# Four weight pieces split on GpSimd in the fourth mixer, and attention scores of both query tiles ahead of their masks in the second and third

## The reference

```python
# second mixer: 8 heads, a part of 128 and a rotated part of 64 in each key
s = einsum(q_nope, k_nope) + einsum(q_rope, k_rope)        # chunk-wise causal mask
# third: 8 heads of two maps of 64 each, causal; softmax(map 0) - lambda * softmax(map 1)
s = einsum('bqhcd,bkhcd->bhcqk', qblk, k) * scale
# fourth: 16 query heads of 64 on 4 key heads, band of 128 keys, with a sink
s = einsum('bnqhgd,bnkhd->bnhgqk', qb, kw) / sqrt(64)
m = max(max(s), sink); e = exp(s - m); p = e / (sum(e) + exp(sink - m))
o = einsum('bnhgqk,bnkhd->bnqhgd', p, vw);  out = o.reshape(B, S, 1024) @ w_o
```

## Time and profile before

| | before |
|---|---|
| median of 3 runs | 1372.0 us (1371.38, 1372.0, 1374.17) |
| the profiled execution, its own time | 1369.26 us |
| its span in the trace | 1367.4 us |
| PE busy | 1337.3 us, 98% of the span |
| PE weight loads busy | 1134.0 us, 83% |
| DVE busy | 892.5 us, 65% |
| ACT busy | 714.7 us, 52% |
| POOL busy | 180.6 us, 13%, nearly all of it in the first 300 us |

### The profile page before, as it was taken

The page is one execution under the profiler, slowest core; times in us unless marked ns, Lnnn a source line. Parts: engine busy times, 40 slices in busy tenths (PEclk is TensorE's granted clock), DMA queues, the critical chain, the costliest instruction groups (busy, mean ns, idle before and its releaser), DMA issues.

```text
span 1367.4 us, 18921 instructions
## 1 busy us (share of the span) xinstructions
PE 1337.3 (98%) x7209; PEld 1134.0 (83%) x7209; DVE 892.5 (65%) x1539; ACT 714.7 (52%) x1217; POOL 180.6 (13%) x327
## 2 busy tenths in 40 slices
PE   9999998999999999999999999999999999999998
PEld 8899897878888888888888887888888877888887
DVE  7886876666555477575554699775554687755553
ACT  7766563345444356454443566564443566544441
POOL 1487888301100000000000000000000000000000
PEclk9999999999999999999999999999999999999999
DMA  9766543346665545266655365066655432566652
GB/s 251 191 160 167 154 123 124 96 126 207 185 189 185 177 145 197 62 201 185 186 186 193 128 210 161 26 210 186 187 188 191 155 123 63 178 192 186 187 191 82
DMA packets 171059, 223.24 MB, mean 163 GB/s; under 512 B 11649, under 2 KB 137402, under 8 KB 170970
## 3 DMA queue, kind: packets, MB, share of 16 engines
q1 hardware_dynamic: 166976, 213.03, 50.4%
q0 software_dynamic: 2224, 7.03, 2.1%
q10 hardware_dynamic: 1770, 1.99, 0.5%
HBM read 217.67 MB, written 4.33 MB: 162 GB/s over the span
## 4 chain that ended last, share of the span: by engine, by line
PE 79%; DVE 13%; ACT 3%; DMA 2%; issue 2%; SPq 0%; ACTq 0%; DVEq 0%
PE psum L959 23%; PE psum L961 22%; PE psum L960 22%; DVE w_low L706 4%; DMA ring<-in_gdn_w_in 2%; PE psum L1192 2%; PE psum L1186 2%; PE psum L1443 1%; PE psum L1403 1%; PE psum L1476 1%; DVE work L2646 1%; DVE arena L2761 1%; ACT w_high L692 1%; PE psum L950 1%; DVE work L878 1%
## 5 line engine op out<-in xcount | busy, mean ns | idle before, releaser
L706 DVE TENSOR_TENSOR w_low<-ring,w_high 128x1024 fp32r<-128x1024 f32 (+3 forms) x395 | 476.7, 1217 | 320.9 <-ACT w_high L692 320.6
L692 ACT ACTIVATE w_high<-ring 128x1024 fp32r<-128x1024 f32 (+3 forms) x395 | 410.6, 1048 | 421.4 <-PE psum L961 402.0
L959 PE MATMUL psum<-w_high,hT 128*128 128x512 f32 (+2 forms) x944 | 371.2, 393 | 0.0
L961 PE MATMUL psum<-w_high,hT 128*128 128x512 f32 (+2 forms) x944 | 366.1, 388 | 0.0
L960 PE MATMUL psum<-w_low,hT 128*128 128x512 f32 (+2 forms) x944 | 365.5, 387 | 0.0
L959 PE MATMUL psum<-w_high,parts 128*128 128x512 f32 (+1 forms) x532 | 210.4, 395 | 1.1 <-DVE parts L2769 1.1
L961 PEld LDWEIGHTS psum<-w_high,hT 128*128 128x128 f32 x944 | 177.2, 188 | 36.5
L961 PE MATMUL psum<-w_high,parts 128*128 128x512 f32 (+1 forms) x532 | 207.0, 389 | 0.0
L960 PE MATMUL psum<-w_low,parts 128*128 128x512 f32 (+1 forms) x532 | 206.8, 389 | 0.0
L960 PEld LDWEIGHTS psum<-w_low,hT 128*128 128x128 f32 x944 | 177.5, 188 | 33.8
L959 PEld LDWEIGHTS psum<-w_high,hT 128*128 128x128 f32 x944 | 177.4, 188 | 33.6
(11 more groups left out here) (303 smaller groups left out, 1395.4 us busy)
## 6 DMA issues: line engine op xcount, KB each, us to landing
ring<-in_ffn_w_gate_up SPq DMA_DIRECT2D x176, 256.0 KB, 3.3
ring<-in_w_gate_up SPq DMA_DIRECT2D x176, 256.0 KB, 3.2
ring<-in_gdn_w_in SPq DMA_DIRECT2D x48, 512.0 KB, 4.7
ring<-in_ffn_w_down SPq DMA_DIRECT2D x44, 512.0 KB, 3.3
ring<-in_w_down SPq DMA_DIRECT2D x44, 512.0 KB, 3.2
ring<-in_da_w_qkv SPq DMA_DIRECT2D x24, 512.0 KB, 4.1
ring<-in_gdn_w_out SPq DMA_DIRECT2D x16, 512.0 KB, 3.4
ring<-in_mla_w_out SPq DMA_DIRECT2D x8, 512.0 KB, 3.7
```

The source lines that it names most:

```text
L692: nc.scalar.activation(piece_slot(w_high, n), piece_slot(ring, n), ACT.Copy).then_inc(s.w_hi, 1)
L706: nc.vector.tensor_tensor(piece_slot(w_low, n), piece_slot(ring, n), piece_slot(w_high, n).bitcast(F32), ALU.subtract).then_inc(s.w_lo, 1)
L959: mm(out, lhs[0], rhs[0], start=start, stop=False)
L961: return mm(out, lhs[1], rhs[0], start=False, stop=stop)
```

## The change

Two things change. In the second and third mixer (`shades_last=True`, the default) a round's scores are issued as: products of both query tiles (in the second mixer the parts of 128 first, then those of 64), then all shades. The fourth mixer (`shades_last=False`) keeps tile 0 with its shades, then tile 1 with its. In the fourth mixer the four pieces named above are split by GpSimd, each by a copy and a subtraction, once `sw_rounds.max` has reached 4 (the maxima of round 3 are known). The four `split_high` of ScalarE and the four `split_low` of VectorE go; both engines wait ahead of their next split until GpSimd's are done.

```diff
-        sw_rounds = Rounds(sem, "sw", ..., HD, q_by)
+        sw_rounds = Rounds(sem, "sw", ..., HD, q_by, shades_last=False)
...
+                def products(i, t, n):
+                    u = i % 2
+                    for j in range(2):
+                        mm(B[2 * u + j][:, keys_of(t)], q(i, j, t)[n], k(i, j, t)[n], start=(n == 0 and (t == 0 or not A.shades_last)),
+                           stop=False, skip_group_check=A.shades_last)
...
+                    if A.shades_last:
+                        for n in parts_:
+                            for t in range(T):
+                                products(i, t, n)
+                        for t in range(T):
+                            last = shaded(i, t)
...
                 if i == 2:
                     empty_bank(act, tp_sq, 5, 1)
-                elif 3 <= i < 7:
-                    split_high(act, a_kv + 5 + i + SPLIT)
             attention(sw_rounds, True, beside_round, last_squares)
             empty_banks(act, tp_so, 1)
+            act.wait_ge(s.w_hi, POOL_SPLITS.stop)
...
                     query_roots(1)
-                elif i < 5:
-                    split_low(dve, a_kv + 5 + i + SPLIT)
-                elif i > 5:
-                    split_low(dve, a_kv + 4 + i + SPLIT)
...
+            dve.wait_ge(s.w_lo, POOL_SPLITS.stop)
...
+            pool.wait_ge(sw_rounds.max, 4)
+            for n in POOL_SPLITS:
+                pool.wait_ge(s.w_hi, n)
+                pool.wait_ge(w_ready[n % RING], landings(n))
+                pool.wait_ge(s.piece_used, n - SPLIT + 1)
+                copy(piece_slot(w_high, n), piece_slot(ring, n)).then_inc(s.w_hi, 1)
+                pool.wait_ge(s.w_hi, n + 1)
+                pool.wait_ge(s.w_lo, n)
+                tt(piece_slot(w_low, n), piece_slot(ring, n), piece_slot(w_high, n).bitcast(F32), ALU.subtract).then_inc(s.w_lo, 1)
```

More of the change, by code:

```diff
@@ L257, with __init__ @@
 class Rounds:
-    def __init__(self, sem, name, rounds, scale, masks, dv, by=None):
+    def __init__(self, sem, name, rounds, scale, masks, dv, by=None, shades_last=True):
         self.rounds, self.scale, self.masks, self.dv, self.by = rounds, scale, masks, dv, by
+        self.shades_last = shades_last
         self.scores = sem(f"{name}_scores")
@@ L453, in program @@
         ffns.append(add_ffn(3, a["w_gate_up_2"][1], a["w_down_2"][1]))
+        POOL_SPLITS = range(a_sout.first - 4 + SPLIT, a_sout.first + SPLIT)
         PROJECTIONS = [pr.first for pr in (a_gout, ffns[0].down, a_lout, ffns[1].down, a_dout, ffns[2].down, a_sout,
@@ L815, in program @@
         da_rounds = Rounds(sem, "da", DA_HEADS, HD ** -0.5, (None, shade_causal), 128)
-        sw_rounds = Rounds(sem, "sw", SW_HEADS // 2, HD ** -0.5, (shade_window, shade_causal), HD, q_by)
+        sw_rounds = Rounds(sem, "sw", SW_HEADS // 2, HD ** -0.5, (shade_window, shade_causal), HD, q_by, shades_last=False)
         def score_banks(u):
@@ L1436, in round_scores @@
             def round_scores(A, q, k):
-                def scores(i):
[L1439 to L1449, removed]
+                def products(i, t, n):
[3 more added lines that the diff above has]
+                           stop=False, skip_group_check=A.shades_last)
@@ new lines, in shaded @@
+                def shaded(i, t):
+                    u = i % 2
+                    for j in range(2):
+                        tiles_ = [(kt, A.masks[1 if kt == t else 0]) for kt in range(t + 1)]
+                        tiles_ = [(kt, shade) for kt, shade in tiles_ if shade is not None]
+                        for n, (kt, shade) in enumerate(tiles_):
+                            last = mm(B[2 * u + j][:, (t + kt) * P:(t + kt + 1) * P], ident_b, shade, start=False,
+                                      stop=(n == len(tiles_) - 1 and (t == T - 1 or not A.shades_last)), skip_group_check=A.shades_last)
+                    return last
@@ new lines, in scores @@
+                def scores(i):
+                    parts_ = range(len(q(i, 0, 0)))
+                    if A.shades_last:
[4 more added lines that the diff above has]
+                            last = shaded(i, t)
+                    else:
+                        for t in range(T):
+                            for n in parts_:
+                                products(i, t, n)
+                            last = shaded(i, t)
```

## The result

| | before | after |
|---|---|---|
| median of six runs each | 1372.21 us (1370.89 to 1374.17) | 1384.78 us (1383.06 to 1387.78) |
| ratio | | 1.0091, 95% interval 1.0078 to 1.0104 |
| span of the profiled execution | 1367.4 us | 1381.0 us |
| fourth mixer: first scores to projection, in the trace | 1116.93 to 1154.54, 37.61 us | 1116.58 to 1168.12, 51.54 us |

The change costs 12.6 us. I had predicted 6.6 (1378.6 us, range 1370 to 1384): the direction was right, the size was half, and the time lies above the upper end of my range. The last row shows where the time is. The fourth mixer is 13.93 us longer, and from its projection to the end of the span both traces need 212.86 and 212.88 us, so nothing behind it is late.

The account below looks back on a forecast made before the run. TensorE, busy 98% of the span, was taken as the bound, nearly even with ScalarE and VectorE in the fourth mixer. Terms 7.8 + 0.7 - 1.2 - 0.7 = 6.6 us over 1372.0 gave 1378.6 us, range 1370 to 1384.

Parts of the forecast that it names:

- stall: Fourth mixer: GpSimd's splits hold VectorE's small operations, so round 4's maxima end 7.8 us late, bounds 0 to 9.6.
- clock: Fourth mixer: TensorE's granted clock drops while it idles and stays low into later rounds, costing 0.7 us, 0 to 1.7.
- splits off ScalarE and VectorE: Fourth mixer: without these splits round 7's turns come sooner, 1.2 us gained, bounds 0.7 to 1.9.
- order of the scores: Second and third mixer: one half-array entry fewer per round, seven rounds counting, 0.7 us gained, 0 to 2.1.
- What bounds it: TensorE, busy 98% of the span; in the fourth mixer's rounds 4 to 6 TensorE, ScalarE and VectorE nearly even.
- the step on the copies: Fourth mixer: five of VectorE's thirteen small operations pass beside GpSimd's second copy; the last ends at 1140.4, not 1135.8.
- the upper bound: Fourth mixer: if copies hold VectorE too, two operations per GpSimd operation, round 4's maxima end at 1148, 9.6 us late.
- The step that the reciprocal would be held: Fourth mixer, round 2: GpSimd's third subtraction holds VectorE's reciprocal of `finished` until 1142.4.
- the first 3.4 us behind the stall: Fourth mixer: a low clock reaching into the rounds after the stall costs up to half of this length.
- No hold: Fourth mixer: GpSimd's long operations don't hold VectorE; only 1.9 us of gains remain, 1370.1 us; chance 0.17.
- VectorE slipping in more often: Fourth mixer: four or more VectorE operations pass between copy and subtraction; stall 2 to 4 us, 1372 to 1374.5; chance 0.10.
- the third rival: Fourth mixer: copies twice as long or VectorE held through subtraction and copy; stall 11 to 13, 1383 to 1387 us; chance 0.06.

Follow-up runs that it names:

- kernel 12: Changed kernel with 3, 46 and 5 unread identity products in TensorE's waits ahead of round 4's scores, round 3's values and round 4's turns; 1378.95 us.
- kernel 8: Changed kernel with GpSimd's splits started after all eight maxima, plus seven unread identity products ahead of round 4's scores and turns; 1368.69 us.
- kernel 11: Kernel before with only the scores' new order, plus seven unread identity products ahead of round 4's scores and turns; 1370.54 us.
- kernel 10: Changed kernel with GpSimd doing only the four copies and the four subtractions back on VectorE; 1381.72 us.
- kernel 5: Changed kernel with GpSimd's splits started once all eight maxima are known instead of the fourth; 1377.73 us.
- kernel 6: Changed kernel with GpSimd's splits started one round later, at the fifth maxima; 1377.92 us.
- kernel 9: Kernel before with only seven unread identity products added, ahead of round 4's scores and turns; 1370.68 us.
- kernel 1: Kernel before with only the scores' new order, splits left on ScalarE and VectorE; 1375.90 us.

## Why the prediction came out at half the loss

The lengths of the mixers in the traces split the loss into terms, each against the one predicted. The sum fell short by 5.8 us: 3.1 of the stall and 3.6 of the clock, less 0.8 that the order of the scores gave more.

| term | predicted us | measured us | from |
|---|---|---|---|
| stall | +7.8 (0 to 9.6) | +10.91 | kernel 12 less kernel 8, 47.29 - 36.38 |
| clock | +0.7 (0 to 1.7) | +4.25 | after less kernel 12, 51.54 - 47.29 |
| splits off ScalarE and VectorE | -1.2 (-1.9 to -0.7) | -1.23 | kernel 8 less kernel 11, 36.38 - 37.61 |
| order of the scores | -0.7 (-2.1 to 0) | -1.50 | second and third mixer, first scores to projection, after less before: 21.15 - 21.88 and 31.40 - 32.17 |
| sum | +6.6 | +12.4 | medians: +12.6 |

The two spans differ by 13.6 us. The 1.1 us that the terms leave is a later start of the second mixer in the trace of after (538.63 against 537.53), ahead of everything that the change touches.

**What bounds it, and the splits taken off.** Both right. Round 7's wait of 0.71 us behind ScalarE's split is gone (0.19 us at 1165.22), and the mixer gets 1.23 us shorter (kernel 8 against kernel 11).

**The stall: the mechanism was right, the step on the copies was wrong.** The hold lasts to the end of GpSimd's instruction, as predicted. The prediction let "five pass beside the second copy", because a two-input operation had passed beside a one-input one of GpSimd's. Copies hold too (0.94 us beside each; kernel 10 with nothing but copies). VectorE's first free moment is then the 0.08 us between a copy and the subtraction behind it, and there are three VectorE operations per pair of 3.43 us: the chain of thirteen ends at 1146.35 and not at the 1140.4 of my layout. I had this case as the upper bound, at 9.6 us, and that was short by 1.3. GpSimd's four pieces took 13.76 us where I had 13.2, which is 0.6 of it. The rest is that I let VectorE do two operations per GpSimd operation, four per pair, and it did three: the whole of GpSimd's time went into the chain of thirteen, and 2.85 us of work were left behind GpSimd's end (1146.10 to 1148.95) where the bound had 2.2. The step that the reciprocal would be held was wrong as well (0.18 us inside a subtraction in kernels 5 and 6); it cost nothing, as GpSimd was done by then. What the prediction took from small operations of 0.5 us for the subtraction, a hold to the end of the instruction, carried over to 2.37 us, within 0.04 us as before.

Two things in the trace of before could have warned me. The operations that passed did so beside GpSimd's TENSOR_SCALAR (again at 252.95 beside one from 252.78 to 253.32), which is not the operation that I moved. And a cast of GpSimd does hold a VectorE operation there, whose like takes 0.16 us at 154.26; the first row is VectorE's, the second GpSimd's:

```profile
285.07 0.26 DVE L2683 TENSOR_SCALAR small<-small 128x8 f32<-128x8 f32 x1 [2.52 <-ACT work L2004]
```

```profile
285.00 0.30 POOL L3369 CAST shades<-consts 128x128 bf16<-128x128 f32 x1
```

It ends at 285.33, the cast at 285.30.

The Trainium skill (SBUF — State Buffer, Who interferes with whom) describes a lock that is held for a whole instruction. The traces agree for copies and subtractions alike: held operations end within 0.04 us of GpSimd's. I set the rule behind one row of the trace of before, and the rule was right for this case. Why that row's operation of two SBUF inputs passed beside a TENSOR_SCALAR stays open. The same section names `tensor_scalar` among the operations that can take the shared pair in a two-port mode, and leaves out a VectorE operation of one SBUF input outside such a mode. The traces agree with both: TENSOR_SCALAR waited (0.62 and 2.20 us), the reciprocal didn't (0.18).

**The clock: the size was wrong, and half of the cause was missed.** The prediction charged a low stretch only with what overlaps the first 3.4 us behind the stall. That length was the step that failed: it lasted 20.5 us, 13.2 of them in rounds where TensorE was busy throughout, and cost 4.25. By the medians it is more, 5.8 us (1384.78 less kernel 12's 1378.95); the profiled execution of after had a clock of 0.988, the three slowest had 0.984 and 0.985. A low stretch without a stall costs more: kernel 5 less kernel 8 is 45.09 - 36.38 = 8.71 us. What I hadn't seen at all is that the kernel before has such executions itself: 31 of its 95 executions had a low clock and took 1373.7 to 1379.4 us. Its one profiled execution, at a clock of 1.00 in this mixer, couldn't show that. With the waits of 0.68 and 0.97 us filled, in kernel 9, none of 12 executions is low and the median is 1370.7. That these waits are the cause is shown by kernels 5 and 8, 1 and 11, where the traces of 5 and 1 also have the low stretch begin behind the wait of 0.97 us; for before it is inferred, since none of its low executions was profiled.

**The order of the scores.** Predicted 3.44 us per round, measured 3.33; the second mixer's rounds went from 4.91 to 4.54 (545.61 to 550.15, where before has 544.51 to 549.42). So more than the entry is saved: 0.21 us per round of the third mixer, inside my 0 to 0.3, and 0.37 in the second, above it. Of the third mixer's gain a part is lost in a new wait of 0.25 us behind VectorE (853.37) and a longer one at the first turns (0.74 us instead of 0.40). The Trainium skill (TensorEngine Tiling (Array Packing), Key Properties) has each change of mode drain the array. The trace agrees in that fewer changes cost less, by the 0.21 and 0.37 us above. What it is worth in the time stays less sure than in the trace: kernel 11 less kernel 9 is -0.14 us by the medians. Seven of kernel 11's executions had a clock of 0.992 or 0.993 and a median of 1370.8 us. Five had 0.996 and a median of 1368.8, which is 1.9 us under the 1370.7 of kernel 9's executions at 0.995 and 0.996. Kernel 8 falls apart in the same way, and its profiled execution (0.992) shows where: the clock is low for 20.5 us in all before 310 us of the trace, in kernel 11's (0.996) for 10.2, and the fourth mixer starts at 1119.79 instead of 1115.64. That is the first mixer, which this change doesn't touch. Why kernel 11 met it in seven executions and kernel 9 in one stays open.

**The chances.** No hold, VectorE slipping in more often: both refuted by the first held operation. The long stall of the third rival, with its clock drop in the rounds, was given 11 to 13 us of stall and 1383 to 1387 us. Those sizes came (10.9 and 1384.8), at a chance of 0.06, but not by that rival's conditions: a copy took 1.04 us and not twice my value, and four pieces took 13.8 us and not 17. What came true of it is that nothing passes between a subtraction and the next copy. The case stood too low because its two parts were taken as one accident, while I had written a long stall down as an upper bound and left the clock with a small term. Whether quarters of the splits would gain at a full clock, why the low stretch lasts 3.4 us in one execution and 30.7 in another, and why taking the splits off made low executions more frequent, stays open.

## What to carry to other kernels

Work moved to GpSimd isn't free for VectorE: give it only stretches in which VectorE reads PSUM, or in which nothing waits for VectorE's small SBUF operations. Where they do meet, count three of them per copy and subtraction (3.43 us here), whatever VectorE's idle time. Where TensorE has short waits in a busy stage, look at the clock of many executions, not of one profile; if they fall into two groups, a few products that nobody reads, put into the waits, can be worth more than the change that one is after (here 2.3 us, and 9 us for kernel 8 against kernel 5). When a prediction hangs on what one engine does beside another, look for the very operation that will be moved, not for one with the same number of inputs. And when several terms of a sum are pushed by the same event, the far case isn't the product of small chances.

## What was unexpected

- GpSimd's copy of 128x1024 from float32 to fp32r took 1.04 us, the subtraction 2.37. In quarters they took 1.43 and 2.80 us, so an instruction more costs about 0.13 to 0.14 us.
- Beside GpSimd's operations VectorE's one-input TENSOR_SCALAR of 128x16 float32 was held too (0.62 and 2.20 us instead of 0.17), the RECIPROCAL (0.18) wasn't.
- Back to back on GpSimd, with a semaphore between, the changed kernel's operations let exactly one VectorE operation of 0.18 us through after each copy, and none after a subtraction.
- The executions of the kernel before fall into two groups by their clock: those at a mean clock of 0.992 or more took 1368.9 to 1375.5 us, the others 1373.7 to 1379.4. Seven products of 0.23 us (46 took 10.49) removed the slower group.
